# One hybrid decoder layer on one core: the transposed input in two transfers, and one attention head's transposes moved ahead of a projection

## The reference

```
h = rms_norm(x, norm_mix_g);  proj = h @ w_in
q_sb, k_sb, v_sb, x_rg, gate_rg, q_ca = split(proj)
o_ca: p = softmax(qh @ kh.T / 8), per head over 256 memory tokens;  o = p @ vh
y = concat([rms_norm(o_sb), rms_norm(o_rg), rms_norm(o_ca)]);  x = x + y @ w_out
x = x + routed(rms_norm(x)) + shared(rms_norm(x))
```

## Time and profile before

| what | value |
|---|---|
| median of 3 runs | 612.72 us |
| the three runs | 610.06, 612.72, 614.21 us |
| profiled execution, its own time | 612.01 us |
| its span in the trace | 610.3 us |
| mean granted TensorE clock | 0.983 of 2.4 GHz |
| PE, DVE, ACT, POOL busy | 569.7, 198.5, 151.2, 20.3 us |
| bytes moved | 227.51 MB, mean 373 GB/s |

### The profile page before, as it was taken

How to read it: one execution, slowest core, us unless ns; L and a number is a source line. 1 busy time by engine, 2 the same in 40 slices (tenths; PEclk the granted TensorE clock), 3 DMA queues, 4 the chain that set the end, 5 groups by cost and what they waited for, 6 DMA issues and landing times.

```text
span 610.3 us, 8237 instructions
## 1 busy us (share of the span) xinstructions
PE 569.7 (93%) x3086; PEld 308.9 (51%) x3087; DVE 198.5 (33%) x527; ACT 151.2 (25%) x299; POOL 20.3 (3%) x78
## 2 busy tenths in 40 slices
PE   7999998999999999995999979999999999989584
PEld 6888774456454444442554425544555444444221
DVE  2337686765344222220222202122212222222102
ACT  4463246343211111110211101111111111111101
POOL 1012131000000000000000000000000000000000
PEclk9999999999999999997999999999999999999988
DMA  8995359732999999999999999999999999999993
GB/s 347 424 407 210 150 212 377 315 124 108 419 414 403 398 423 420 420 421 420 423 420 422 422 420 418 421 421 422 422 423 420 419 420 422 422 420 422 420 390 113
DMA packets 33993, 227.51 MB, mean 373 GB/s; under 512 B 3872, under 2 KB 4000, under 8 KB 8480
## 3 DMA queue, kind: packets, MB, share of 16 engines
q1 hardware_dynamic: 33808, 226.93, 90.5%
q10 hardware_dynamic: 144, 0.03, 0.0%
HBM read 225.90 MB, written 1.05 MB: 372 GB/s over the span
## 4 chain that ended last, share of the span: by engine, by line
PE 57%; SPq 28%; DMA 7%; ACT 3%; issue 2%; DVE 2%; DVEq 0%; ACTq 0%
SPq L354 22%; PE ps L1576 17%; PE ps L1598 9%; PE ps L1544 6%; PE ps L1336 6%; PE ps L1606 5%; DMA cell_gu<-in_w_gu_e 4%; PE ps L1458 4%; PE ps L1353 4%; SPq L450 2%; SPq L454 2%; DMA cell_d<-in_w_down_e 2%; SPq L435 2%; DMA x_in<-in_x 1%; PE ps L1343 1%
## 5 line engine op out<-in xcount | busy, mean ns | idle before, releaser
L1576 PE MATMUL ps<-cell_gu,xg 128*64 128x512 f32 (+2 forms) x1056 | 205.5, 621 | 20.8 <-DMA cell_gu<-in_w_gu_e 20.7
L1576 PEld LDWEIGHTS ps<-cell_gu,xg 128*64 128x64 f32 (+2 forms) x1056 | 66.4, 133 | 153.9 <-issue 153.6
L1598 PE MATMUL ps<-cell_d,e_hT 128*64 128x512 f32 (+2 forms) x528 | 102.2, 597 | 2.1 <-DMA cell_d<-in_w_down_e 1.3
L1282 DVE SCALAR_TENSOR_TENSOR ylo<-ps,gslot,yhi 128x512 fp32r<-128x512 f32 x56 | 42.1, 751 | 127.3 <-ACT yhi L759 127.3
L1223 DVE TENSOR_TENSOR e_h<-e_sg,ps 128x256 f32<-128x256 f32 x28 | 11.8, 421 | 178.7 <-ACT e_sg L747 178.7
L759 ACT ACTIVATE yhi<-ps,gslot 128x512 fp32r<-128x512 f32 x56 | 38.5, 687 | 125.5 <-PE ps L1598 125.5
L747 ACT ACTIVATE e_sg<-ps 128x256 f32<-128x256 f32 x28 | 10.8, 385 | 207.3 <-PE ps L1576 207.3
L1598 PEld LDWEIGHTS ps<-cell_d,e_hT 128*64 128x64 f32 (+2 forms) x528 | 30.8, 128 | 58.0 <-issue 55.4
L1544 PE MATMUL ps<-pick,xhi 128*128 128x256 f32 x224 | 48.8, 299 | 1.4 <-DVE pick L1140 1.4
L1606 PE MATMUL ps<-yhi,S 128*128 128x512 f32 x112 | 46.5, 415 | 0.6 <-DVE ylo L1282 0.6
L1544 PEld LDWEIGHTS ps<-pick,xhi 128*128 128x128 f32 x224 | 34.4, 189 | 22.0 <-issue 21.7
(11 more groups left out here) (310 smaller groups left out, 466.5 us busy)
## 6 DMA issues: line engine op xcount, KB each, us to landing
cell_gu<-in_w_gu_e SPq DMA_DIRECT2D x128, 1024.0 KB, 26.3
cell_d<-in_w_down_e SPq DMA_DIRECT2D x60, 1024.0 KB, 26.3
wA<-in_w_qk SPq DMA_DIRECT2D x8, 512.0 KB, 10.4
wo<-in_w_out SPq DMA_DIRECT2D x1, 4096.0 KB, 13.5
cell_d<-in_w_down_e SPq DMA_DIRECT2D x8, 512.0 KB, 17.4
wR<-in_w_rest SPq DMA_DIRECT2D x3, 1024.0 KB, 28.1
wV<-in_w_v SPq DMA_DIRECT2D x1, 2048.0 KB, 17.5
w_kv<-in_w_mem SPq DMA_DIRECT2D x1, 2048.0 KB, 26.8
```

The lines of the kernel that those rows point to most:

```text
L1282: nc.vector.scalar_tensor_tensor(ylo[:, c], ps[:, Y[half], :], gslot[:, g.index % 2:g.index % 2 + 1], yhi[:, c].bitcast(F32), ALU.mult, AL ...
L1576: last = mm(ps[side * w:(side + 1) * w, U, :], rows(k, slice(side * w, (side + 1) * w)), cell_gu[i][:, k - k0, :], start=k == 0, stop=k == ...
L1598: last = mm(ps[side * w:(side + 1) * w, Y[half], :], e_hT[:, kk, side * w:(side + 1) * w], cell_d[n][:, kk, half * 512:(half + 1) * 512], ...
```

## The change

The transfer of `xT_in` is cut in two by k (0 to 3 and 4 to 7), each 0.5 MB, with its own semaphore; `wA[0]` is issued between them. ACT and DVE wait for the second half ahead of k = 4 and k = 6. The transfers of `wA[1]`, `x_in` and all after them keep their order. Later, in PE's order, unit 27 (the four transposes of cross-attention head 0) stands ahead of `project(1)` and not behind it. `project(1)` is four parts of k, so four products. Nothing of the computation is altered.

```
-            sp.dma_start(xT_in[:], x_t).then_inc(xT_loaded, 16)
+            sp.dma_start(xT_in[:, 0:4, :], x_t[:, 0:4, :]).then_inc(xT_loaded, 16)
             for n in range(8):
                 sp.dma_start(wA[n][:], w_qk[n]).then_inc(wA_loaded[n], 16)
+                if n == 0:
+                    sp.dma_start(xT_in[:, 4:8, :], x_t[:, 4:8, :]).then_inc(xT_more_loaded, 16)
                 if n == 1:
                     sp.dma_start(x_in[:], x[0].rearrange("(t p) d -> p t d", p=P)).then_inc(x_loaded, 16)
...
             for k in ACT_K:
+                if k == 4:
+                    act.wait_ge(xT_more_loaded, 16)
                 nc.scalar.mul(hT[:, k, :], xT_in[:, k, :], vec[:, MIX + k:MIX + k + 1]).then_inc(xT_act, 1)
...
             for k in DVE_K:
+                if k == 6:
+                    dve.wait_ge(xT_more_loaded, 16)
                 nc.vector.tensor_scalar(hT[:, k, :], xT_in[:, k, :], vec[:, MIX + k:MIX + k + 1], None,
                                         ALU.mult).then_inc(xT_dve, 1)
...
             project(0, (3,))
             unit(26)
+            unit(27)
             project(1)
-            unit(27)
             unit(28)
             project(2)
```

More of the change, by code:

```diff
@@ L256, in hybrid_decoder_layer @@
         (
-            xT_loaded, memT_loaded, x_loaded, mem_loaded, vec_loaded, wg_loaded, wV_loaded, kv_loaded, wo_loaded, x1_loaded,
+            xT_loaded, xT_more_loaded, memT_loaded, x_loaded, mem_loaded, vec_loaded, wg_loaded, wV_loaded, kv_loaded, wo_loaded, x1_loaded,
             rt_loaded, rb_loaded, consts, zeroed, ssq_act, std_act, xn_dve, diag_dve, row_ps, row_act,
@@ L269, in hybrid_decoder_layer @@
         ) = [ctx.enter_context(nc.semaphore(name)) for name in """
-            xT_loaded memT_loaded x_loaded mem_loaded vec_loaded wg_loaded wV_loaded kv_loaded wo_loaded x1_loaded             rt_loaded rb_loaded consts zeroed ssq_act std_act xn_dve diag_dve row_ps row_act xT_act xT_dve
+            xT_loaded xT_more_loaded memT_loaded x_loaded mem_loaded vec_loaded wg_loaded wV_loaded kv_loaded wo_loaded x1_loaded             rt_loaded rb_loaded consts zeroed ssq_act std_act xn_dve diag_dve row_ps row_act xT_act xT_dve
             unit_ps unit_act unit_dve conv_dve z_ps bc_act mask_pool w_dve
```

## The result

The changed kernel takes 615.92 us in the median of its runs, the kernel before 612.29 us beside it. The ratio is 1.0072, with a 95% interval from 1.0058 to 1.0086: slower by 3.6 to 4.4 us, within the 1% taken as no change. Forecast was 614.0, or 614.7 from the median. One execution of each kernel lies far outside (3295.15 us before, 2040.36 us after); the two stand in the medians and not in the ratio, and leaving them out moves neither median by more than 0.13 us. The profiled execution of the changed kernel took 613.81 us, its span is 612.1.

A forecast was written before the change was run, and what follows sets the result against it. The prediction took a PE, ACT and DVE chain to about 150 us, then an expert-weight stream, as the bound. 0 + 0.8 + 1.2 = +2.0 us on 612.01 gives 614.0; range 610.0 to 617.0 for eight in ten.

The forecast's parts named there:

- That the front decides: Up to about 150 us: a microsecond won or lost ahead of the expert-weight stream is won or lost at the end.
- Part 1, no gain from PE's earlier start: Halved xT_in at the start: PE begins 1.3 us sooner, but the row step still waits for x_in; gain 0.
- its own sign of being wrong: At the start: the prediction is wrong if the row step moves from 14.5 to 14.6 us.
- 0.5 MB takes 1.26 us, counted back from the landing of the whole: Start of the queue: at 415 GB/s the halves of xT_in would land at 4.6 and 5.9 us before the change.
- the price of smaller transfers: Start of the queue: 0.5 MB transfers in place of 1 MB cost 0, as the queue is full at 415 GB/s.
- my bounds of 0 and 1.7 us: Start of the queue: the price of a 0.5 MB transfer lies between 0 and 1.7 us.
- Rival 3: At the start: smaller transfers or the added issue make x_in late, moving the row step; up to 615.7 us, chance 0.09.
- The fixed 2.0 us per DMA: At the start: if this skill figure came on top, x_in would be 2.0 us late; the prediction argued against it.
- Rival 2, the clock at the start: First 32 products: if the clock rises late, PE's earlier start gives back up to 1.3 us; 611.5 or 612.7, chance 0.11.
- Part 2: Unit 27 ahead of project(1): 2.13 us of waiting for DVE replaces 1.31 us ahead of unit 28; +0.8 us.
- The clock behind the wait: Behind unit 27's wait near 100 us: PE's clock falls to half, costing 1.2 us.
- My upper bound of 1.7: Behind unit 27's wait: up to 3.4 us at half clock, so at most 1.7 us lost.

The follow-up runs named there:

- part 2 alone: Kernel before with only unit 27 moved ahead of project(1), xT_in in one transfer: median 615.78 us, ratio 1.0040.
- unit 27 in the middle with both edits: Kernel before with unit 27 inside project(1), one more warm-up product and two idle-time products ahead of the second router product: 610.50 us, ratio 0.9981.
- part 1 alone: Changed kernel with unit 27 put back behind project(1), xT_in still in two halves: median 612.68 us, ratio 1.0010.
- the filled kernel: Changed kernel with four products nobody reads added between unit 26 and unit 27: median 613.56 us, ratio 1.0017.
- the second measurement: The changed kernel run again unaltered, for a second profile: median 615.58 us, ratio 1.0048 to the kernel before.
- unit 27 in the middle: Kernel before with unit 27 placed behind the first two of project(1)'s four products: medians 612.87 and 612.55 us, ratios 1.0018 and 1.0011.
- the same products without the move: Kernel before with one more warm-up product and two idle-time products near 134 us, unit 27 where it was: 611.24 us, ratio 1.0000.

## Why the prediction was right or wrong

*That the front decides.* Right in the main. From SP's first ranked load to the end of the span it is 460.2 us in the kernel before, 460.1 in the changed one, 459.1 in its second profile and 459.8 in that of before. It was not always so: 458.3 (part 2 alone) and 462.7 (unit 27 in the middle with both edits). The stream adds or takes up to 2.5 us of its own, for reasons left open.

*Part 1, no gain from PE's earlier start.* Right that nothing of it arrives, with another path than forecast: PE never started 1.3 us sooner, and the row step moved, which the prediction named as its own sign of being wrong. The term "0.5 MB takes 1.26 us, counted back from the landing of the whole" failed: the first half landed at 5.65 and not at 4.6. At the start the queue moves less than the 415 GB/s of the earlier trace rows. From 2.5 to 4 us it was 310 to 373 GB/s in the seven profiles with one transfer in packets of 8 KB and 240 to 281 in the four with halves by k around `wA[0]`; from 4 to 5 us 407 to 451 against 266 to 287. The full queue from which I took 0 for the price of smaller transfers is there with two transfers only after 5 us. The price was within my bounds of 0 and 1.7 us: 0.8 us on `x_in`. Rival 3 was therefore true in its mechanism. The Trainium skill's warning against transfers under 1 MiB (DMA: Bandwidth & Descriptors, section Bandwidth) pointed the right way here. The fixed 2.0 us per DMA that the prediction took from the Trainium skill (the same page, section Anatomy of one DMA — SWDGE (gpsimd) path) were, as an estimate of the price here, too high: `x_in` was 0.8 us late in the mean.

*Rival 2, the clock at the start.* Given 0.11, and the rise came late in six of the 14 profiles, with a fall of the same effect in a seventh; what it decides is whether part 1 loses or wins. It and rival 3 nearly cancel, and I had treated them as alternatives. They are both true at once. So that part 1 alone measured 0.5 us, close to the 0 of the forecast, is luck. The Trainium skill's statement that the moment of the rise differs from run to run (TensorE: Matmul & The Clock Gate, Part 1: The HAM clock gate) is borne out: the 32 products took 7.17 to 7.64 us in seven profiles and 9.07 to 9.98 in the six with a late rise.

*Part 2.* Right: wait 2.23 for 2.13, next projection +0.8 us, the wait ahead of unit 28 gone. (The prediction counts the projections from the end of the unit ahead, 0.16 us behind their starts in the rows, before and after alike; the difference is not touched by it.)

*The clock behind the wait.* Right in its mechanism, the term was sized too small. It fell in two of the three profiles with an unfilled wait; it cost 1.66 us in one and 3.0 in the other, since it can stay down for 6.8 us and not 3.4. My upper bound of 1.7 was read from one fall, and the same trace has a longer one, behind PE's wait of 6.3 us for expert weights: (0.14 + 0.50 + 0.04) x 5 x 2 = 6.8 us.

```profile
275.00:280.00 5.00, 0.01 (x2) 0.00 (x0) 0.00 (x0) 0.00 (x0) 0.00 (x0) 0.86 1.02 423
280.00:285.00 5.00, 3.68 (x20) 1.15 (x24) 0.00 (x0) 0.00 (x0) 0.00 (x0) 0.50 1.02 423
285.00:290.00 5.00, 5.00 (x40) 3.30 (x33) 1.34 (x3) 1.59 (x4) 0.00 (x0) 0.96 1.01 419
```

By the filled kernel the clock costs 2.0 us in the median against 1.2 forecast.

*The sum.* Forecast 0 + 0.8 + 1.2 = 2.0. Measured by removal: part 1 0.5 us (612.68 against 612.14, within noise), the clock 2.0, and what is left of the 3.5 us of the second measurement (615.58 against 612.07) is 1.0, for which the trace gives 0.8. So the change cost 3.6 us by the medians where 2.0 was forecast: the direction and the mechanism of part 2 were right, and most of what is missing is the term of the clock. Part 2 alone does not fit as well: its 3.6 us leave 2.8 for the clock, or 1.6 by its ratio.

What stays open: why two transfers make `x_in` late, since neither packet size nor order alone explains it; and why unit 27 in the middle, whose front is 0.9 us shorter in the trace, was no faster in two measurements. For that the record speaks for the clock. The mean granted clock over twelve executions is 0.9813 and 0.9809 in its two measurements, against 0.9829 and 0.9836 over the 35 of before beside them: 1.0 and 1.7 us of full speed less, as much as the front gained or more. The mean counts falls in the stream of experts too, where PE waits for weights anyway, so where the falls that cost time lie is not shown. The kernel with the added products is 2.0 us faster, which fits, but the same products without the move gave nothing by the ratio.

## What to carry to other kernels

Moving an operation up in an in-order queue moves the wait for its input up too: compare when the input is ready with when the queue would get there, and if there is divisible work beside it, split that work around it (here this made the front 0.9 us shorter in the trace and no difference in the median). A quiet stretch of PE can cost twice, once as waiting and once as half clock behind it. Look also at what stands ahead of the wait (here 0.65 us of waiting and four products with one column), and if the wait can't be avoided, fill it with products that nobody reads. At the very start of this kernel the rate of its steady stretches did not hold, so a transfer cut in two there must be priced from the first microseconds.

## What the runs showed of the hardware that had not been expected

- Between 2.5 and 4 us the queue moved 373 GB/s with 1 MB as one first transfer, 251 with the same bytes as two transfers by k, and 224 with two of 64 partitions each, with the DMA share at 0.84 to 0.95 in all three. Single profiles differ: one transfer in packets of 8 KB gave 310 to 373, in packets of 4 KB 254.
- The same 32 products at the start take 7.2 to 7.6 us in some executions and 8.9 to 10.0 in others, and a longer warm-up did not end that: 9.30 us in one of the two profiles with five warm-up products.
- At unit 27, behind waits of about the same length (2.23, 2.25, 2.25 us), the clock stayed at 2.4 GHz once, fell once so that project(1) lost 1.66 us, and once so that PE lost 3.0 us.
- A fall came behind a wait of only 1.0 us too, at 138 to 145 us among products of 64 columns, in three of the twelve profiles of kernels without the added products there.
